# A hybrid encoder layer on one core: a second decay buffer, ScalarE in the convolution, a router on raw rows, another order of steps

## The reference, cut to what matters

```
h = RMSNorm(x); z, xbc, dt, q, k, v, u = split(h @ W_in)
xbc = silu(depthwise_conv(xbc))                 # 768 channels, 4 taps
y_ssd = Mamba2 scan, forward and backward, 8 heads, chunks of 128 tokens,
        gated by silu(z), RMSNorm per group
y_na  = 2-D neighbourhood attention on q, k, v  # 4 heads, RMSNorm on q and k
y_pool = centred mean pooling of u, 4 windows
x += [y_ssd | y_na | y_pool] @ W_out
x += cross attention(RMSNorm(x), RMSNorm(mem))  # 4 heads, 256 memory rows
hn = RMSNorm(x); group logits (4) and expert logits (32) = hn @ W_router + b
x += sum over the top-2 experts of the top-1 group of gate * MLP_e(hn)
```

## Time and profile before

| what | value |
|---|---|
| runs, median of 3 | 1178.75 us (1177.96 to 1183.33) |
| profiled execution, own time | 1180.71 us |
| its span, first to last instruction | 1178.7 us |
| mean granted clock of TensorE | 0.939 |
| busy: PE, DVE, ACT, POOL | 86%, 67%, 40%, 26% |

### The profile page before, as it was taken

How to read it: one execution, slowest core, us unless ns; L and a number is a source line. 1 busy time by engine, 2 the same in 40 slices (tenths; PEclk the granted TensorE clock), 3 DMA queues, 4 the chain that set the end, 5 groups by cost and what they waited for, 6 DMA issues and landing times.

```text
span 1178.7 us, 13976 instructions
## 1 busy us (share of the span) xinstructions
PE 1017.5 (86%) x5029; PEld 808.7 (69%) x5029; DVE 784.9 (67%) x1251; ACT 466.0 (40%) x849; POOL 301.5 (26%) x346
## 2 busy tenths in 40 slices
PE   4898798998898999999979999667999888888983
PEld 3676586767677778788867888555776666666661
DVE  5437776777677677862355676457987777778771
ACT  5123343323234323421234343224665564655640
POOL 2223314221341222200111111004342232343322
PEclk9899999897898989899989999867999999999997
DMA  6132223121132523325110113734899998998962
GB/s 227 46 108 63 81 96 113 46 79 56 47 102 68 169 81 126 108 66 193 57 57 18 54 54 134 285 135 156 343 375 349 349 367 333 362 351 345 363 247 89
DMA packets 63396, 197.40 MB, mean 167 GB/s; under 512 B 16416, under 2 KB 22976, under 8 KB 50912
## 3 DMA queue, kind: packets, MB, share of 16 engines
q1 hardware_dynamic: 43344, 152.73, 35.6%
q0 software_dynamic: 18688, 39.52, 9.4%
q10 hardware_dynamic: 1296, 4.26, 0.9%
HBM read 190.16 MB, written 37.75 MB: 193 GB/s over the span
## 4 chain that ended last, share of the span: by engine, by line
PE 40%; DVE 15%; DMA 11%; issue 10%; ACT 7%; POOL 3%; ACTq 0%; DVEq 0%; POOLq 0%
DMA edr<-w_e_down 10%; PE bank L943 6%; PE bank L944 6%; PE bank L945 6%; DVE egl L1727 3%; PE gu_ps L943 2%; PE gu_ps L945 2%; PE gu_ps L944 2%; PE y_ps L1324 2%; PE bank L1128 2%; PE bank L1010 2%; ACT ghi L1394 1%; PE xg_ps L1289 1%; ACT dec L1570 1%; ACT prob L1588 1%
## 5 line engine op out<-in xcount | busy, mean ns | idle before, releaser
L943 PE MATMUL bank<-Wh,hTh 128*128 128x512 f32 x384 | 160.6, 418 | 7.9 <-issue 6.7
L944 PE MATMUL bank<-Wl,hTh 128*128 128x512 f32 x384 | 155.1, 404 | 0.0
L945 PE MATMUL bank<-Wh,hTl 128*128 128x512 f32 x384 | 154.5, 402 | 0.0
L1727 DVE TENSOR_TENSOR egl<-egr,ghi 128x2048 fp32r<-128x2048 f32 x64 | 143.9, 2288 | 14.9 <-ACT ghi L1394 14.9
L1394 ACT ACTIVATE ghi<-egr 128x2048 fp32r<-128x2048 f32 x64 | 119.5, 1930 | 0.0
L943 PE MATMUL gu_ps<-ghi,xgH 128*128 128x512 f32 x256 | 103.8, 406 | 1.4 <-DVE xgL L2092 1.4
L945 PE MATMUL gu_ps<-ghi,xgL 128*128 128x512 f32 x256 | 101.0, 395 | 0.0
L944 PE MATMUL gu_ps<-egl,xgH 128*128 128x512 f32 x256 | 100.7, 393 | 0.0
L943 PEld LDWEIGHTS bank<-Wh,hTh 128*128 128x128 f32 x384 | 76.2, 198 | 25.0 <-issue 7.4
L1394 ACT ACTIVATE dhi<-edr 128x1024 fp32r<-128x1024 f32 x32 | 33.9, 1060 | 136.1 <-DMA edr<-w_e_down 120.3
L945 PEld LDWEIGHTS bank<-Wh,hTl 128*128 128x128 f32 x384 | 75.4, 196 | 16.8
(11 more groups left out here) (325 smaller groups left out, 2249.0 us busy)
## 6 DMA issues: line engine op xcount, KB each, us to landing
egr<-w_e_gate SPq DMA_DIRECT2D x32, 1024.0 KB, 17.9
egr<-w_e_up SPq DMA_DIRECT2D x32, 1024.0 KB, 21.1
edr<-w_e_down SPq DMA_DIRECT2D x32, 1024.0 KB, 14.5
raw<-w_in SPq DMA_DIRECT2D x50, 256.0 KB, 3.0
xn<-w_in SPq DMA_DIRECT2D x22, 256.0 KB, 3.0
x_sb<-x_prompt SPq DMA_DIRECT2D x8, 512.0 KB, 6.0
partial_rows<-x_sb ACTq DMA_DIRECT2D x8, 512.0 KB, 2.6
ffn_rows<-xn_ffn POOLq DMA_DIRECT2D x8, 512.0 KB, 2.9
```

What stands on the lines that cost most here:

```text
L943: pe.matmul(dst, ah, bh, start=first, stop=False)
L944: pe.matmul(dst, ah, bl, start=False, stop=False)
L945: return pe.matmul(dst, al, bh, start=False, stop=last)
L1727: tt(egl[n % 4][:, a, :, :], egr[n % 4][:, a, :, :], ghi[n % 2][:, a, :, :].bitcast(F32), ALU.subtract)\
```

## The change

- A second decay buffer lies over `prob` and `probT`; chunks alternate. `ssd_groups` issues the decay of chunk c + 2 behind `sy c`. `xdt` and `yn` (the normalisation that ended `sy`) become steps of their own. DVE waits where the buffer collides with the softmax.
- The convolution's first product goes to ACT as an Identity with scale and bias; tanh and the last DVE operation become the step `act`.
- The router transposes `x_sb` itself, its weights are multiplied by the gain once, and its logits by the row's root. `norm ffn` now only feeds the rows that the experts gather; their store moves to `router` on POOL.
- The gain of the first norm is loaded behind the first weight quarter; `hT` steps move up between the first loads; PE waits for the constants at `dtp 0`.
- The rest of `dtv` after the logarithm becomes `dtw`. Mixer steps and the routing loop stand in another order.

```diff
@@ timeline(), first loads
             tl += [("norm", "mix", 0), ("w", U_QK, 0), ("norm", "mix", 1), ("w", U_QK, 1), ("hT", "mix", 0),
-                   ("norm", "mix", 2), ("w", U_QK, 2), ("norm", "mix", 3), ("w", U_QK, 3)]
-            tl += [("hT", "mix", i) for i in range(1, TPS)]
+                   ("norm", "mix", 2), ("w", U_QK, 2), ("hT", "mix", 1), ("norm", "mix", 3), ("w", U_QK, 3),
+                   ("hT", "mix", 2)]
+            heads[0].insert(1, ("hT", "mix", 3))
@@ timeline(), convolution
-        mixed([[u[0]], [conv[4], na1[0]], [conv[5], conv_t[4]] + (ssd_groups(s - 1)[-1] if s else []),
-               [na2[0], u_t[0], u[1], nav[0]]], quarters(u0 + U_XS))
-        mixed([[na1[1], conv[0]], [conv[1], conv_t[0], na2[1]]], quarters(u0 + U_Z))
-        tl += [u_t[1], ("dtv", s), norm[0], conv[2], nav[1], conv_t[1], na1[2], norm[1], conv[3], conv_t[2]]
-        mixed([[z[0], h_t[0], na2[2]], [z[1], h_t[1], norm[2], nav[2], na1[3]],
-               [z[2], h_t[2], ("dt", s), conv_t[3], norm[3], na2[3]], [z[3], ("sback", s, 3), nav[3], h_t[3]]],
+        mixed([[u[0], na1[0]], [conv[4]], [act[4], conv[5], conv_t[4]] + (ssd_groups(s - 1)[-1] if s else []),
+               [act[5], na2[0], u_t[0], u[1], nav[0]]], quarters(u0 + U_XS))
+        mixed([[na1[1], conv[0]], [act[0], conv[1], conv_t[0], na2[1]]], quarters(u0 + U_Z))
+        tl += [act[1], conv[2], conv_t[1], u_t[1], nav[1], ("dtv", s), act[2], na1[2], conv[3], norm[0], ("dtw", s), act[3],
+               norm[1]]
+        mixed([[z[0], conv_t[2], h_t[0], na2[2]], [z[1], h_t[1], norm[2], nav[2], na1[3], ("dt", s)],
+               [z[2], h_t[2], conv_t[3], norm[3], na2[3]], [("sback", s, 3), z[3], ("sback", s, 2), nav[3], h_t[3]]],
@@ timeline(), routing loop
-        tl += on(i, ("xs2", i)) + on(i + 2, ("hT", "xa", i + 2)) + on(i + 1, ("hn3", "xq", i + 1))
+        tl += on(i + 2, ("hT", "xa", i + 2)) + [("xs2", i)] + on(i + 1, ("hn3", "xq", i + 1))
+        if i == NT - 1:
+            tl += [("hT", "ffn", i - 1)]
+        tl += [("xav", i)] + on(i + 1, ("xs1", i + 1))
+        if i < NT - 1:
+            tl += on(i - 1, ("hT", "ffn", i - 1)) + [("xsn", i + 1)] + on(i + 2, ("hn1", "xq", i + 2), ("hn2", "xq", i + 2))
+        tl += ranked + on(i - 1, ("norm", "ffn", i - 1))
+        if i == NT - 1:
+            tl.append(("pre", 0))
+        tl += on(i - 1, ("router", i - 1), ("topk", i - 1)) + [("xo", i)] + on(i + 3, ("norm", "xa", i + 3))
+    i = NT - 1
+    tl += [("norm", "ffn", i), ("hT", "ffn", i), ("rank", i - 1), ("slots", i - 1), ("router", i), ("pre", 1), ("topk", i),
+           ("rank", i), ("slots", i)]
@@ ssd_groups(s)
-    back = [[("sback", s, 1), dec[0]]]
-    return back + [[y[0]], [dec[1], out[0]], [y[1]], [dec[2], out[1]], [y[2]], [dec[3], out[2]], [y[3]], [out[3]]]
+    groups = [[("sback", s, 1), dec[0], x[0]], [dec[1]]]
+    for c in range(TPS):
+        groups.append([y[c]] + x[c + 1:c + 2])
+        groups.append(dec[c + 2:c + 3] + [yn[c], out[c]])
+    return groups
@@ PE
-                if kind == "init":
+                if step == ("dtp", 0):
                     pe.wait_ge(const_ld, 16 * N_CONST)
@@ ACT
+                    act.activation(cacc[:, k % 2, :], pb(step)[:, :], ACT.Identity, scale=cwh[:, m, 1:2],
+                                   bias=cbh[:, m:m + 1]).then_inc(conv_in, 1)
+                elif kind == "act":
@@ DVE
-                    link(ts(acc, b[:, :], cwh[:, m, 1:2], cbh[:, m:m + 1], ALU.mult, ALU.add))
+                    dve.wait_ge(conv_in, k + 1)
+                        tt(router_w[:, :, :], router_w[:, :, :], per_head(g_ffn, NL), ALU.mult).then_inc(router_g, 1)
-                    tt(logits[:, i, :], pb(step)[:, 0:NL], router_b[:, :], ALU.add).then_inc(is_free(step), 1)
+                    stt(logits[:, i, :], pb(step)[:, 0:NL], rs[:, k:k + 1], router_b[:, :], ALU.mult, ALU.add)\
+                        .then_inc(is_free(step), 1)
+                    if k:
+                        dve.wait_ge(t_done, k)
+                    if k > 1:
+                        wait_full(dve, ("sy",) + chunks[k - 2], 0)
+                    if c == 1:
+                        wait_full(dve, ("nav", s, 3))
```

More of the change, by code:

```diff
@@ L126, in timeline @@
     xo = quarters(U_XO)
[L127 to L131, removed]
+    tl += [("gain", "ffn"), ("hn1", "xq", 0), ("hn2", "xq", 0), ("out", "out", TPS + 3, 1), ("hn3", "xq", 0),
+           ("hT", "xa", 1), ("norm", "xa", 2), xo[0], xo[1], ("xs1", 0), ("xsn", 0), ("hn1", "xq", 1), ("hn2", "xq", 1),
+           xo[2], xo[3]]
@@ L132, in on @@
+    for i in range(NT):
         def on(j, *steps):
             return list(steps) if 0 <= j < NT else []
-        routed = on(i - 2, ("topk", i - 2))
         ranked = on(i - 2, ("rank", i - 2), ("slots", i - 2))
-        tl += on(i, ("xs2", i)) + on(i + 2, ("hT", "xa", i + 2)) + on(i + 1, ("hn3", "xq", i + 1))
[L138 to L153, removed]
+        tl += on(i + 2, ("hT", "xa", i + 2)) + [("xs2", i)] + on(i + 1, ("hn3", "xq", i + 1))
[8 more added lines that the diff above has]
+        tl += on(i - 1, ("router", i - 1), ("topk", i - 1)) + [("xo", i)] + on(i + 3, ("norm", "xa", i + 3))
@@ L166, in ssd_groups @@
 def ssd_groups(s):
[L168 to L170 removed]
+    dec, x, y, yn, out = ([(kind, s, c) for c in range(TPS)] for kind in ("sdec", "xdt", "sy", "yn", "sout"))
+    groups = [[("sback", s, 1), dec[0], x[0]], [dec[1]]]
[3 more added lines that the diff above has]
+    return groups
 def bank_uses(step):
@@ L478, in encoder_layer @@
         stk.close()
+        decays = [dec, nc.alloc_sbuf_tensor_at("dec1", [P, 2, SSD_H, P], F32, offset=at["prob"])]
         oneh_p = nc.alloc_sbuf_tensor_at("oneh_p", [P, 2 * NT, P], BF16, offset=at["raw0"])
@@ L1127, in _ @@
                         for dr in range(2):
-                            last = pe.matmul(b[:, hc], dec[:, dr, h, :], xdt[:, dr, hc], start=dr == 0, stop=dr == 1)
+                            last = pe.matmul(b[:, hc], decays[c % 2][:, dr, h, :], xdt[:, dr, hc], start=dr == 0, stop=dr == 1)
                     last.then_inc(is_full(step, 0), 1)
@@ L1442, in _ @@
                         dst = normed(st, i)
-                        if before_it:
+                        if st == "xa" and before_it:
                             wait_full(act, before_it[-1], 1)
-                        else:
+                        elif not (st == "ffn" and i):
                             wait_raw_used(act, plan.last_in[2 if st == "xa" else 3])
@@ L1569, in _ @@
                             for h in range(4 * hh, 4 * hh + 4):
-                                last = act.activation(dec[:, dr, h, :], dec[:, dr, h, :], ACT.Exp,
-                                                      bias=ncs[:, dr, c, h:h + 1])
+                                d = decays[c % 2][:, dr, h, :]
+                                last = act.activation(d, d, ACT.Exp, bias=ncs[:, dr, c, h:h + 1])
                             last.then_inc(e_done, 1)
@@ L1585, in _ @@
                         wait_transposed(act, k)
+                        if step[1] == 0:
+                            wait_full(act, ("sy", SEQS - 1, TPS - 1), 0)
                     for j in range(4):
@@ L1821, in _ @@
                     ins.then_inc(conv_sum, 1)
+                elif kind == "act":
+                    m, k = step[2], nth("conv", *step[1:])
                     dve.wait_ge(conv_th, k + 1)
@@ L2316, in _ @@
                                 .then_inc(router_ld, 16)
-                elif kind == "hT" and step[1] == "ffn":
-                    i = step[2]
+                elif kind == "router":
+                    i = step[1]
                     pool.wait_ge(xn_done, 1 + nth("norm", "ffn", i))
```

67 lines of the change are left out of this document (43 added, 24 removed).

## The result

The changed kernel takes 1231.07 us (median; 1227.45 to 1232.1), the kernel before 1179.03 in the same runs: ratio 1.044 (95% interval 1.041 to 1.047). It is 52 us slower where the forecast was 7 us faster. The profiled execution took 1227.45 around a span of 1225.4, 46.7 us more span than before; I account for these 46.7.

The account below looks back on a forecast made before the run. The prediction took the mixer as a PE queue interrupted by late DVE steps. Terms of -23.6 us at full clock plus 17 for lower clock gave -6.6: 1174.1 us profiled, 1172 in the runs, range 1149 to 1197 (8 in 10).

Parts of the forecast that it names:

- the sum: Whole span: stage terms of -23.6 us at full clock plus 17 for lower clock, giving -6.6 us.
- First loads: Before the first convolution: constants awaited later and first product started earlier, -11.5 us (bounds -8, -12).
- Recurrence: Two recurrence stages: waits for the decay go, `sout` waits for `yn` instead; +3.7 and +3.5 us.
- 82.8 of work: First recurrence: PE work that, with stalls of 5.4, 13.9, 3.4 and 3.3, made 108.8 us.
- Convolution: Two convolution stages: shorter stalls in the new order; first 91.7 us instead of 104.2, -12.5, second sequence -11.
- The second sequence: Convolution stage of the second sequence: claimed to gain -11 us, beside -12.5 for the first.
- Loop: Routing loop: passes of 25.3 us instead of 20.7, +18 over four passes; net +4.2 with the tail.
- the tail: Last routing passes and tail up to the gather: 54 us instead of 68.1, -14.
- the gain's multiplication: Router weights times gain, once, 128 x 320: falls into DVE slack; without slack it costs 0.5 us.
- Clock: About 16 stops over 2 us: 1.4 us each in the mixer, 0.6 in the loop, +17 in all.
- Rival 3: Whole kernel slower: lower clock behind 16 stops, 2.2 us each, takes 35 us against 23.6; 1190 us, chance 0.27.
- Overlap of the second buffer: Second decay buffer over `prob` and `probT`: waits at `nav 3`, `na1 0` and `xs1 0` costed at nothing.

Follow-up runs that it names:

- the run with all three old orders: Changed kernel with recurrence one chunk ahead, routing loop and convolution stages in their old orders; start, ScalarE first product, raw-row router, second buffer remain: 1145.7 us, ratio 0.972.

## Why the prediction was wrong

The span came out 53 us above the sum. By the table, the recurrences are 32.5 us above their terms, the convolutions 27.1 and loop and tail 11.8; the 17 us put down for the clock come off, since the rows hold it already.

**First loads: right** (-11.2 for -11.5), with the third head product at 32.13 as walked.

**Recurrence: the step that failed most.** The mechanism was the one written down: `yn c` behind `dec c+2`, `sout` waiting for it, one stop over 10 us (11.9; I had 13.9), the third head product late on `hn2` (4.6 for 5.4). The size was not, and two terms carry that. First, stops: I walked 26.0 and 14.2 us, measured are 32.3 and 25.9. In sequence 0 the walk gave about 3.3 us, the least possible, to each `sout` behind the worst; the runs show that the look-ahead also takes `dec 3` from under `sout 2`, which then waits 9.1 us (9.9 with `yn` first). Second, I set "82.8 of work" against a stage of 105.1 in which PE was busy for 93.95. The difference is work at the lower clock, and it did not go: PE is busy for 92.08 with the new order. Busy time of the row plus my stops would have made 120 of that stage, beside 124.4 measured. In sequence 1, where 5.8 us of lower clock were taken off, the same sum makes 131.9 beside 143.1: there the stops, put at 14.2, were the larger miss.

**Convolution: failed.** "Stalls of 0.4, 1.1, 4.3 and 1.2 in place of 15.3" became 1.1, 3.2, 4.5 and 4.9, 13.7 in all, and the waits of `convT`, which I had gone, are 9.4 us in four (11.1 before). `hT 0` was right. Missed were the two weight splits ahead of `act 0` and POOL's queue ahead of `sback 3`, whose old cover, `z 3`, I let go at 1.2 us. I also read "each `convT` one product later" into the new list, where that holds for `convT 2` alone. And of the -12.5 only 8.3 were stops; the other 4.2 were lower-clock work taken as gone, while PE was busy for 88.57 us before and 88.49 after. The second sequence, put at -11 by analogy and not walked, came to +5.7. That DVE loses twelve products is true and moved little that PE waited for (`convT` 9.4 us with it, 11.5 without).

**Loop: right in kind.** Passes of 25.3 us were forecast; the four measured from one `hT xa` to the next last 30.0, 25.4, 26.3 and 25.6, with `hT xa` waiting up to 3.63 for 4; the tail gave -11.9 for -14. Two misses: the gain's multiplication, "falls into slack of DVE", stands behind a head root and made a stop of 4.11 us, with half clock behind it, in the pass of 30.0; and of the tail's gain I gave 4 us to what DVE does behind the last addition, while the run with all three old orders, where that order is the old one, has the same tail. It came with the raw router rows; the order is not needed for it.

**Clock: wrong in the mixer, short in the loop.** I had at least 21 us of the mixer's lower-clock work vanish (4.2, 11.2 and 5.8 in three of its stages) and put back 12.6 us for nine stops. There were seventeen stops over 2 us, where the kernel before had ten, and PE's busy time in the four mixer stages went from 398.9 to 398.1: neither the loss nor the return shows. The mean granted clock fell from 0.87 to 0.83 in recurrence 0, but that mean includes the idle time. Rival 3 had the right sign by a mechanism that these rows refute there; in the loop, where the clock went from 0.98 to 0.91, busy time did grow, by 11.3 us; loop and tail together by 8.4, where I had put 4.2, and by 12.8 over the run with all old orders, which has the same router. The Trainium skill (TensorE: Matmul & The Clock Gate, "HAM oscillation") describes a loop whose every wait is paid again as cold work, that is, at the lower clock. The loop here agrees; the mixer, with clocks of 0.87 to 0.96 before the change, does not, and no run shows why the two differ.

**Overlap of the second buffer** with `prob`: costed at nothing, and PE has no wait for `na1 0` or `xs1 0`.

## What to carry over

Move a step in a list that all engines share only after naming, for each queue, what now stands between the result and its reader: here 0.6 us of `yn` went behind 7 us of decay and cost 24 us. Looking further ahead moved cover here, it did not make any; ask which stop at the end of the loop loses its own. And forecast from PE's busy time as the rows have it plus the stops: that would have brought the first recurrence to 120 us instead of 108.8, at 124.4 measured. It does not save a stage whose stops were not walked through every queue: the second convolution, taken by analogy, missed by 16.7 us.

## What the runs showed of the hardware

DVE and POOL hold each other up. `yn`, two operations on 128 x 256, takes 0.61 us alone; in the kernel before it took 2.17 while POOL made `xdt`, as long as POOL's 2.09 (DVE, POOL):
```profile
248.43 2.17 DVE L1917 TENSOR_SCALAR y<-y,yrs 128x256 f32<-128x256 f32 x2 [2.04 <-POOL yrs L2272]
...
248.36 2.09 POOL L2381 TENSOR_TENSOR xdt<-x_sb,dts 128x512 f32<-128x512 f32 x2
```
Four of eight `yn` there took 2.17 to 2.19 us, each beside `xdt`. The other way round, POOL's two operations of `xdt`, 2.04 us at 218.80, took 3.02 at 272.01 in the run with `xdt` behind the decay, where DVE's weight split began beside them. The Trainium skill (SBUF — State Buffer, "SBUF: two separate sides") calls the port pair that the two share an exclusive lock, which for some kinds of DVE operation is held for the whole instruction; these rows agree, and that the time was lost to the lock is a reading of them, which no run isolates. ScalarE's Identity with a scale and a bias per partition took 0.76 to 0.78 us on 128 x 512 from PSUM, where its plain copy takes 0.60; the trace has six table loads, as many as before.
